# Feature-major q and k projections with an in-SBUF half swap, in a one-core transformer layer

## What is computed

```python
def rope(x, pos):
    ...
    x1, x2 = xf[..., :half], xf[..., half:]
    return jnp.concatenate([x1 * cos - x2 * sin, x2 * cos + x1 * sin], axis=-1).astype(x.dtype)

def input_projection(h, w_in, b_in, a_ln_g, a_ln_b, pos):
    z = h @ w_in + b_in
    u, va, q, k, vb, gate_a, gate_b = jnp.split(z, IN_SPLITS, axis=-1)
    u = jax.nn.gelu(u)
    va = layer_norm(jax.nn.gelu(va), a_ln_g, a_ln_b)
    q = rope(q.reshape(bn, L, nh, HEAD_DIM), pos)...
    k = rope(k.reshape(bn, L, nh, HEAD_DIM), pos)...

for g, (window, dilation) in enumerate(((128, 1), (512, 4), (2048, 16))):
    o, lse = dilated_attention_prompt(q[:, :, g], k[:, :, g], vb[:, :, g], dilation, window // dilation)
    kv_rows.append(jnp.stack([kg[:, -keep:], vg[:, -keep:]], axis=2))   # keep = min(window, 1024)
```

## Time and profile before

| | |
|---|---|
| median of 3 runs | 1572.88 us (1571.16 to 1574.89) |
| the profiled execution, whole | 1572.88 us |
| its span, first to last instruction | 1571.1 us |
| TensorE busy | 1516.7 us (97%) |
| VectorE, ScalarE, GpSimd busy | 942.6, 805.3, 356.2 us |
| granted TensorE clock, mean | 0.988 |
| first block (attention and projections) | to 443.4 us |
| gates and mixing | 443.4 to 883.9 us |
| experts | from 883.9 us |

### The profile page before, as it was taken

The page is one execution under the profiler, slowest core; times in us unless marked ns, Lnnn a source line. Parts: engine busy times, 40 slices in busy tenths (PEclk is TensorE's granted clock), DMA queues, the critical chain, the costliest instruction groups (busy, mean ns, idle before and its releaser), DMA issues.

```text
span 1571.1 us, 26976 instructions
## 1 busy us (share of the span) xinstructions
PE 1516.7 (97%) x9227; PEld 1341.4 (85%) x9228; DVE 942.6 (60%) x1171; ACT 805.3 (51%) x1059; POOL 356.2 (23%) x396
## 2 busy tenths in 40 slices
PE   7999999999999999998999899999999999999986
PEld 7998998899999899997886788888888888888864
DVE  6325324522335336284665799898986686678957
ACT  5128315612922222353223387888866575678843
POOL 0550082055042000000000253323322222223210
PEclk9999999999999999999999899999999999999998
DMA  6221311222162663573531699999997696699958
GB/s 221 72 66 41 95 52 52 78 85 82 49 217 89 183 116 119 192 225 93 191 130 56 221 371 381 373 379 376 383 390 242 246 386 240 249 363 366 380 228 326
DMA packets 166405, 329.99 MB, mean 210 GB/s; under 512 B 18063, under 2 KB 63417, under 8 KB 165817
## 3 DMA queue, kind: packets, MB, share of 16 engines
q1 hardware_dynamic: 152456, 300.21, 54.4%
q0 software_dynamic: 11568, 20.28, 4.2%
q10 hardware_dynamic: 2304, 8.46, 1.4%
HBM read 300.27 MB, written 49.97 MB: 223 GB/s over the span
## 4 chain that ended last, share of the span: by engine, by line
PE 49%; DVE 2%; ACT 1%; DMA 1%; issue 1%; ACTq 0%; POOLq 0%; DVEq 0%
PE psum L2239 24%; PE psum L2271 12%; PE psum L2136 7%; PE psum L2222 2%; PE psum L2130 1%; PE psum L2248 1%; PE psum L2159 1%; PE psum L2147 0%; DVE expert_lo L2023 0%; DMA expert_rows<-block_out,block_out_rows 0%; DMA expert_raw<-in_w_down_dram 0%; DMA block_rows<-moe_input,slot_table 0%; DVE first_rows L2115 0%; DVE first_rows L2112 0%; ACT square_junk L1878 0%
## 5 line engine op out<-in xcount | busy, mean ns | idle before, releaser
L2023 DVE TENSOR_TENSOR expert_lo<-expert_raw,expert_hi 128x2048 fp32r<-128x2048 f32 x190 | 425.0, 2288 | 73.8 <-ACT expert_hi L1811 73.7
L1811 ACT CAST expert_hi<-expert_raw 128x2048 fp32r<-128x2048 f32 x190 | 350.7, 1903 | 33.8 <-issue 16.7
L719 PE MATMUL psum<-w_hi,h_T_hi 128*128 128x256 f32 (+1 forms) x792 | 228.6, 289 | 3.1 <-DVE h_T_lo L579 2.4
L2239 PE MATMUL psum<-expert_hi,block_T_hi 128*128 128x512 f32 x576 | 228.1, 396 | 2.4 <-DVE block_T_lo L2036 2.4
L2239 PE MATMUL psum<-expert_hi,block_T_lo 128*128 128x512 f32 x576 | 225.3, 391 | 0.0
L2239 PE MATMUL psum<-expert_lo,block_T_hi 128*128 128x512 f32 x576 | 224.7, 390 | 0.0
L719 PE MATMUL psum<-w_hi,h_T_lo 128*128 128x256 f32 (+1 forms) x792 | 221.9, 280 | 0.0
L719 PE MATMUL psum<-w_lo,h_T_hi 128*128 128x256 f32 (+1 forms) x792 | 221.9, 280 | 0.0
L719 PEld LDWEIGHTS psum<-w_hi,h_T_hi 128*128 128x128 f32 (+1 forms) x792 | 140.1, 177 | 10.3 <-issue 4.5
L719 PEld LDWEIGHTS psum<-w_lo,h_T_hi 128*128 128x128 f32 (+1 forms) x792 | 140.3, 177 | 2.4
L719 PEld LDWEIGHTS psum<-w_hi,h_T_lo 128*128 128x128 f32 (+1 forms) x792 | 140.2, 177 | 2.5
(11 more groups left out here) (305 smaller groups left out, 2834.4 us busy)
## 6 DMA issues: line engine op xcount, KB each, us to landing
expert_raw<-in_w_gate_dram SPq DMA_DIRECT2D x64, 1024.0 KB, 9.9
expert_raw<-in_w_up_dram SPq DMA_DIRECT2D x64, 1024.0 KB, 8.5
expert_raw<-in_w_down_dram SPq DMA_DIRECT2D x64, 1024.0 KB, 9.3
w_raw<-in_w_in_dram SPq DMA_DIRECT2D x21, 1024.0 KB, 6.4
gate_logits<-gate_logits_out ACTq DMA_DIRECT2D x16, 516.0 KB, 2.6
gate_logits_even<-gate_logits SPq DMA_DIRECT2D x8, 516.0 KB, 4.3
gate_logits_odd<-gate_logits SPq DMA_DIRECT2D x8, 516.0 KB, 4.4
x_in<-in_x_prompt_dram SPq DMA_DIRECT2D x8, 512.0 KB, 5.0
```

The costliest lines, as they stand in the source:

```text
L719: m = nc.tensor.matmul(dst, st, mv, start=(k == 0 and n == 0), stop=(k == KD - 1 and n == 2))
L1811: nc.scalar.copy(weh[:, u], wraw[:, SLOT[u]]).then_inc(s_uh[m], 1)
L2023: nc.vector.tensor_tensor(wel[:, u], wraw[:, SLOT[u]], weh[:, u].bitcast(F32), ALU.subtract).then_inc(s_ul[m], 1)
L2239: m = nc.tensor.matmul(bank(m_), x_, w_, start=(u == 0 and k == 0 and i == 0), stop=(u == 1 and k == 3 and i == 2))
```

## The change

The q and k chunks are projected the way of u: the weights stand still and the tokens move, in pieces of 352, 352 and 328, so that a chunk has six steps and its result comes with features on partitions. The order of the steps, the places of the attention and of the weight splits relative to the chunks stay as they were.

- ACT, at the end of each q or k step, copies PSUM with the bias column into `zf` (ring of three), waits for that copy, and starts four transfers on its own queue that bring the halves of each head, swapped, into `zs` (32 partitions each, 352 or 328 floats in a partition).
- DVE, one iteration later, multiplies `zf` with the cosines and `zs` with the signed sines, now laid out with features on partitions, and adds them into `qT` or `kT`, sorted by residue. The third piece has a fourth instruction for the 8 sample tokens. DVE no longer adds q's and k's bias, and GpSimd has no work in this block.
- The cosines and sines are loaded twice over (four transfers with runs of 256 bytes, 1152 KB, where one had runs of 512 bytes and 576 KB), turned by PE in steps 6 to 10 (18 transposes in PSUM bank 2, five groups) and copied by ACT into `cosT` and `sinT`, two copies a group. The bias row load of the second chunk at the start goes away.
- The 48 pairs of transposes of q and k go away. The keys to be kept and the sample rows are turned back to rows: a list `TURNS` of 16 entries, one in each step from the first attention step of a group on (2 in group 0, 5 in group 1, 9 in group 2). PE does a turn behind the projection of its step and ahead of the attention's matmuls, ACT copies it one iteration later, SP stores it. All turns use PSUM bank 2, so a turn waits until ACT has copied the one before it (`s_kr`).
- SP waits for no q or k row any more.

Cut to its core, the diff is:

```diff
+    elif CHUNKS[_c][0] in "qk":
+        STEPS += [(_c, n, j) for j in range(3) for n in range(2)]
...
+KEPT_COLS = [[7], [2 * n + 1 for n in range(4)], list(range(NT))]
+TURNS = []
+for _g in range(NG):
+    TURNS += [(FIRST_STEP[4 * _g + 3] + 1 + _n, _g, _t) for _n, _t in enumerate([None] + KEPT_COLS[_g])]
+TURN_AT = {at: n for n, (at, _, _) in enumerate(TURNS)}
+KEPT_POS = {n: m for m, n in enumerate(n for n, (_, _, t) in enumerate(TURNS) if t is not None)}
+COS_AT = 6
...
+                for w in range(2):
+                    for half in range(2):
+                        sp.dma_start(cs[:, :, w, DH * half:DH * half + DH],
+                                     a["c_rope"][0].rearrange("t p c -> p t c")[:, :, DH * w:DH * w + DH]) \
+                          .then_inc(s_cs, 16)
...
+                def store_turned(n):
+                    _, g, t = TURNS[n]
+                    sp.wait_ge(s_kr, n + 1)
+                    if t is None:
+                        for which in range(2):
+                            sp.dma_start(new_d[3 * g + which], qks[:, which, :]).then_inc(s_qs, 16)
+                        sp.dma_start(kv_s[g][:, 0], qks[:, 1, :]).then_inc(s_qs, 16)
+                    else:
+                        m = KEPT_POS[n]
+                        sp.dma_start(turned_rows(kv_p[g][:, 0], g, t), rot[:, m % 3, :]).then_inc(s_ro[m % 3], 16)
...
+                    if i in QPOS:
+                        c, n, j = STEPS[i]
+                        m = QPOS[i]
+                        w = TJ[j][1] - TJ[j][0]
+                        f = CHUNKS[c][2] // P + n
+                        act.wait_ge(s_pj, i + 1)
+                        if m == 0:
+                            act.wait_ge(s_bcol, 1)
+                        if m >= 3:
+                            act.wait_ge(s_qk, ADDED[m - 2])
+                        nc.scalar.activation(zf[:, m % 3, 0:w], bank(i % 2)[:, 0:w], ACT.Identity,
+                                             bias=bcol[:, f:f + 1]).then_inc(s_fm, 1)
+                        act.wait_ge(s_fm, FPOS[i] + 1)
+                        for q in range(4):
+                            to, of = slice(32 * q, 32 * q + 32), slice(32 * (q ^ 1), 32 * (q ^ 1) + 32)
+                            nc.scalar.dma_start(zs[to, m % 3, 0:w], zf[of, m % 3, 0:w]).then_inc(s_zs[m % 3], 16)
+                    if 0 <= i - 1 - COS_AT < 5:
+                        f = i - 1 - COS_AT
+                        w = min(2 * P, TOK - 2 * P * f)
+                        act.wait_ge(s_csT, f + 1)
+                        nc.scalar.copy(cosT[:, 2 * P * f:2 * P * f + w], bank(2)[:, 0:w]).then_inc(s_cst, 1)
+                        nc.scalar.copy(sinT[:, 2 * P * f:2 * P * f + w], bank(2)[:, 2 * P:2 * P + w]).then_inc(s_cst, 1)
+                    if i - 1 in TURN_AT:
+                        n = TURN_AT[i - 1]
+                        _, g, t = TURNS[n]
                         act.wait_ge(s_rT, n + 1)
-                        g = CHUNKS[c][1]
-                        nc.scalar.copy(place_cols(dst[:], g, t),
-                                       by_residue(bank(2)[:, 0:2 * P].rearrange("p (a q) -> p a q", a=2), g)) \
-                            .then_inc(s_qk, 1)
+                        if t is None:
+                            if g:
+                                act.wait_ge(s_qs, 48 * g)
+                            nc.scalar.copy(qks[:].rearrange("p w c -> p (w c)"), bank(2)[0:NS, :]).then_inc(s_kr, 1)
+                        else:
+                            m = KEPT_POS[n]
+                            if m >= 3:
+                                act.wait_ge(s_ro[m % 3], 16 * (m // 3))
+                            nc.scalar.copy(rot[:, m % 3, :], bank(2)[:, 0:HW]).then_inc(s_kr, 1)
...
+                    if i - 1 in QPOS:
+                        c, n, j = STEPS[i - 1]
+                        kind, g, _ = CHUNKS[c]
+                        m = QPOS[i - 1]
+                        t0, t1 = TJ[j]
+                        z, y = zf[:, m % 3, 0:t1 - t0], zs[:, m % 3, 0:t1 - t0]
+                        to = (qT if kind == "q" else kT)[:, n, :]
+                        if m == 0:
+                            dve.wait_ge(s_cst, 10)
+                        dve.wait_ge(s_fm, FPOS[i - 1] + 1)
+                        dve.wait_ge(s_zs[m % 3], 64 * (m // 3 + 1))
+                        nc.vector.tensor_tensor(z, z, cosT[:, t0:t1], ALU.mult).then_inc(s_rp, 1)
+                        nc.vector.tensor_tensor(y, y, sinT[:, t0:t1], ALU.mult).then_inc(s_rp, 1)
+                        dve.wait_ge(s_rp, 2 * m + 2)
+                        wp = min(t1, SEQ) - t0
+                        if g == 0:
+                            parts = (to[:, t0:t0 + wp], z[:, 0:wp], y[:, 0:wp])
+                        else:
+                            nr = 4 if g == 1 else NT
+                            parts = (to[:, 0:SEQ].rearrange("p (r i) -> p r i", r=nr)[:, :, t0 // nr:(t0 + wp) // nr],
+                                     z[:, 0:wp].rearrange("p (i r) -> p r i", r=nr),
+                                     y[:, 0:wp].rearrange("p (i r) -> p r i", r=nr))
+                        nc.vector.tensor_tensor(*parts, ALU.add).then_inc(s_qk, 1)
+                        if j == 2:
+                            nc.vector.tensor_tensor(to[:, SEQ:TOK], z[:, wp:wp + NS], y[:, wp:wp + NS],
+                                                    ALU.add).then_inc(s_qk, 1)
...
+                        elif kind in "qk":
+                            t0, t1 = TJ[j]
+                            dst = bank(i % 2)[:, 0:t1 - t0]
+                            xs = (hh[:, k, t0:t1], hl[:, k, t0:t1])
+                            H_, L_ = H_[:, t * P:(t + 1) * P], L_[:, t * P:(t + 1) * P]
+                            trio = ((H_, xs[0]), (H_, xs[1]), (L_, xs[0]))
...
-                    if i >= 2 and i - 2 in TPOS:
-                        n = TPOS[i - 2]
-                        pe.wait_ge(s_rope, ROTPOS[i - 2] + 1)
+                    if 0 <= i - COS_AT < 5:
+                        f = i - COS_AT
+                        pe.wait_ge(s_cs, 64)
+                        if f:
+                            pe.wait_ge(s_cst, 2 * f)
+                        for t in range(2 * f, min(2 * f + 2, TILES)):
+                            rt = rows(t)
+                            for w in range(2):
+                                at = 2 * P * w + P * (t - 2 * f)
+                                m = nc.tensor.transpose(bank(2)[:, at:at + rt], cs[0:rt, t, w, :], ident[0:rt, 0:rt])
+                        m.then_inc(s_csT, 1)
+                    if i in TURN_AT:
+                        n = TURN_AT[i]
+                        _, g, t = TURNS[n]
+                        pe.wait_ge(s_qk, 16 * (g + 1))
                         if n:
-                            pe.wait_ge(s_qk, n)
+                            pe.wait_ge(s_kr, n)
                         for pair in range(2):
-                            m = nc.tensor.transpose(bank(2)[:, pair * P:(pair + 1) * P],
-                                                    rot[:, RPOS[i - 2] % 3, pair * P:(pair + 1) * P], ident[:])
+                            if t is None:
+                                for w, of in enumerate((qT, kT)):
+                                    m = nc.tensor.transpose(bank(2)[0:NS, HW * w + P * pair:HW * w + P * pair + P],
+                                                            of[:, pair, SEQ:TOK], ident[:])
+                            else:
+                                m = nc.tensor.transpose(bank(2)[:, pair * P:(pair + 1) * P],
+                                                        kT[:, pair, t * P:(t + 1) * P], ident[:])
```

More of the change, by code:

```diff
@@ L85 @@
 NSTEP = len(STEPS)
+TJ = ((0, 352), (352, 704), (704, TOK))
 FIRST_STEP = [min(i for i, s in enumerate(STEPS) if s[0] == c) for c in range(NC1)]
@@ L286, in build @@
         s_fm = sem("feature_rows_ready")
-        s_rope = sem("rotated_ready")
-        s_rT = sem("rotated_transposed")
+        s_rp = sem("rotation_terms")
+        s_zs = [sem(f"halves_swapped{i}") for i in range(3)]
+        s_csT = sem("cos_sin_transposed")
+        s_cst = sem("cos_sin_T_ready")
+        s_rT = sem("keys_turned_back")
+        s_kr = sem("key_rows_ready")
+        s_qs = sem("sample_q_k_stored")
+        s_vs = sem("sample_v_stored")
         s_qk = sem("qk_T_ready")
-        s_ro = [sem(f"rotated_stored{i}") for i in range(3)]
+        s_ro = [sem(f"key_rows_stored{i}") for i in range(3)]
         s_vo = [sem(f"v_rows_stored{i}") for i in range(4)]
@@ L306, in build, with bias_loads @@
         s_pool = sem("pool_chain")
[L309 to L323 removed]
         def v_stored(n):
             return sum(1 + keeps(m // NT, m % NT) for m in range(n % 4, n + 1, 4))
[L329 to L333 removed]
+        QK = [i for i, s in enumerate(STEPS) if CHUNKS[s[0]][0] in "qk"]
+        QPOS = {s: n for n, s in enumerate(QK)}
+        ADDED = [0]
+        for i in QK:
```

(12 more changed lines are left out.)

142 lines of the change are left out of this document (38 added, 104 removed).

## The result

| | before | after |
|---|---|---|
| median | 1572.32 us (1571.16 to 1574.89, 4 runs) | 1605.88 us (1602.73 to 1607.41, 4 runs) |
| ratio | | 1.0209, 95% interval 1.0198 to 1.0221 |
| span of the profiled execution | 1571.1 us | 1602.8 us |
| TensorE busy | 1516.7 us | 1513.7 us |
| granted TensorE clock, mean | 0.988 | 0.975 |

The change costs 33.6 us, 2.1%. All of it is in the first block, which ends 33.5 us later. The part behind it takes 1.8 us less.

The account below looks back on a forecast made before the run. TensorE's work and waits were taken as the bound: -21.5 (work) + 27.1 (turn waits) + 5.3 (cosines) + 3.5 (start) on 1572.88 gave 1587.3, plus 4.5 for the clock: 1591.8 us; own range 1578 to 1605, with rivals 1574 to 1606.

Parts of the forecast that it names:

- TensorE's work: q and k chunks: fewer matmuls -17.1 us, transpose pairs gone -10.3, added turns and cosine transposes +5.9; together -21.5 us.
- The turn's wait: Attention steps of the first block: TensorE waits 13 times until ACT has copied the turn before; +27.1 us.
- The cosines: Steps 9 and 10: ACT's cosine copies stand behind its bias copy and four transfer issues; 2.6 us twice, +5.3 us.
- The start: Start of the kernel: cosine transfers in 256-byte runs delay the fourth tile of x; +3.5 us (1.6 to 5.6).
- The clock: Behind five new waits of 3.4 to 3.9 us the clock drops to half; 5 x 0.9 = +4.5 us (0 to 9).
- the clock takes more: Rival: half-clock spells cover whole steps and also follow the cosines' 2.6 us waits, 7 x 3 us: 1608 us; chance 0.06.
- The swap lands late: Rival: half-swap transfers land after 5 us, not 1.8; +2.9 at k0 and k1, +1.0 at k2: 1598.6 us; chance 0.10.
- The waits are cheap: Rival: ACT's copy of the turn is done when PE comes; 1560.2 us, decided at 0.98 us mean wait; chance 0.10.
- no change: Rival: waits at the turns come to half the predicted size; 1573.8 us with the clock held; chance 0.08.

Follow-up runs that it names:

- three small edits: Changed kernel with the turns behind the scores, ACT's cosine copies first, and the cosines loaded once and doubled by GpSimd: 1553.36 us, ratio 0.9875 to the kernel before.

## Why the prediction was right, point by point

The forecast was 1591.8 us, the time is 1605.88: the right side, but 14 us low. The range that I gave last, 1574 to 1606, holds it by 0.1 us, and that is luck: the range of my own terms, 1578 to 1605, does not, and the last one reaches higher only for a rival to which I gave 0.06. In the block the sum had +18.9 us, and the profile shows +33.5.

| | predicted | measured |
|---|---|---|
| columns and transpose pairs of q and k | -27.4 | -27.1 |
| work added: turns; cosine transposes | +4.0; +1.9 | +2.8; +2.2 |
| idle time at the turns | +27.1 | +24.4 |
| idle time at the cosines | +5.3 | +7.9 |
| idle time at the start | +3.5 | +1.5 |
| work at half clock | +4.5 | +21.9 |

The measured side is worked out so. Six chunks of q and k held 162.9 us of work before, and would hold 6 x 22.63 without the cosines. The idle time of the four attention chunks went from 6.8 to 31.2 us. Their busy time went from 161.9 to 180.2 us; with the turns behind the scores, at full clock, it is 164.7, so the turns' work is 2.8 and the clock 15.6. In q0 the busy time is 27.65 at 0.86 and 23.59 at 1.00: 4.1. In v0 35.71 and 33.45: 2.3. Sum +33.6.

The split between idle time and clock in the attention chunks is one of accounts, not of causes. With TensorE kept busy and the clock up, these chunks became only 7.6 us shorter, where 15.6 are booked to the clock; the rest came as waiting, and as 3.4 us at half clock behind a late swap. So in time the half clock cost from 14 us (7.6 + 4.1 + 2.3) to 21.9, and 4.5 is too little by either.

- **TensorE's work** was right. A chunk of 144 matmuls takes 22.63 us, 0.157 us for each, where I had 22.8. The trace keeps to its own spacing and not to that of the Trainium skill ("TensorE: Matmul & The Clock Gate", Back-to-back issue gap), by an estimate from which (109 ns) a chunk would have taken 15.7 us.
- **The turn's wait**, the largest term, was right in place and mechanism, and nearly in size: 3.60, 3.62, 3.60 and 3.80 us where I had 3.5 and 3.9; 1.26 where I had 2.55; 0.99 to 1.69 in group 2 where I had 1.6; 3.30 at the weight split where I had 3.4. The one of 2.55 was priced from rows of the kernel before, in which the gelu of va starts 1.80 us behind the projection's end; in this step of the changed kernel it starts 0.44 us behind it.
- **The cosines** failed in one number. I took an issue on ACT's queue at 0.33 us, from a transfer of 516 KB with 128 partitions; an issue of these 32-partition transfers inside SBUF takes 0.64 us (2.55 for four). It is 0.31 x 4 = 1.2 us more for each wait: 4.0 where I had 2.6. My upper bound of 7 us assumed 0.5 and was passed, at 7.9.
- **The start** cost 4.9 us, of which the x tile is 1.5 of idle time and 2.3 of half clock; the cosine transposes make the rest. Runs of 256 bytes moved at 204 to 232 GB/s between 16 and 20 us, those of 512 bytes at about 290: 19 ns for a run, against 28. The middle that I took between 14 and 28 was near, and the x tile came 2.7 us later (ACT goes on at 23.02 instead of 20.35). Only 1.5 us of that became idle time, since other waits of v0 became shorter: that of its last step went from 1.99 to 1.17 us. The Trainium skill ("DMA: Bandwidth & Descriptors", Specifications) puts the edge at 512 bytes. The trace shows a slope instead: 512-byte runs are also well under the 393 GB/s of longer ones, and half the length costs a further quarter of the rate, not half of it.
- **The clock** is the step that failed, 4.5 us where 21.9 came. I counted five spells, of 4 us each, behind the waits of over 3 us, and took 1.8 us for a spell and half of that as hidden. These five came, 27.3 us long together in place of 20. I had left out four more: two at the cosines (10.2 us), one at the x tile (6.8) and one behind the shorter waits of u0 (3.4). That makes nine, 47.8 us long together. Half of the time at the lower level was lost: 30.7 us in the attention chunks cost 15.6 of busy time. The Trainium skill ("TensorE: Matmul & The Clock Gate", HAM oscillation — how this bites in real kernels) has the same half in its sum, and this trace agrees. That part of it lies beside ACT's loop was right: filling the idle time gave back 7.6 of the 15.6 us there. My rival "the clock takes more", 1608 us at 0.06, is nearest to what happened, and its chance was too small: its ground, that the spells also follow the waits at the cosines, could have been taken from the sum itself.
- **The swap lands late** did not decide: a landing takes 2.0 us in the median, I had 1.8, and the first turns waited 0.3 and 1.0 us. It is fragile, though: in two of the variants the first turn of va0 waited 2.3 us, and in one of them that of va1 3.2.
- **The waits are cheap** was wrong for this kernel, where the mean wait was 28.9 / 13 = 2.2 us; so was **no change**, which needed half of my size. The bound of 0.98 us agrees with the one other point there is: with a mean wait of 3.5 / 13 = 0.3 us the kernel with the turns behind the scores is no slower than the kernel before.

## What to carry to other kernels

Where a step is handed back and forth between two engines, look whether the partner's answer stands behind all of its other work of the iteration. If it does, try the consumer at the end of the iteration: here that alone gave back 37 us. A wait of TensorE can cost more than its length. In these profiles every wait of over 3 us in the steps of this block had a stretch at half clock with it, and one of about 1.5 us sometimes did. Price such a stretch as half of the work in it, count all the waits in the sum, and ask which part lies beside another engine's loop. When the work that a change saves is real, as the 27 us here, look for what it left on the way before undoing it: three small edits made 1.0209 into 0.9875.

## What had not been expected of the hardware

- An issue of a transfer between two places of SBUF, 32 partitions of 1408 bytes, holds ACT's queue for 0.61 to 0.64 us and SP's for 0.61, where one of a 516 KB transfer held it for 0.33.
- Waits of 1.69, 1.50 and 1.50 us in steps some 8 us apart were followed by 3.4 us at a granted clock of 0.50, where a single one of 1.48 us was not the earlier trace rows. In the variants single waits of 1.69 and 1.56 us were followed by it, and others of 1.51, 1.55 and 1.56 us were not.
- GpSimd doubled the cosines (three copies of 128 x 576) between 18 and 21 us without any effect on the other engines' steps that the profile shows.
